# VectorE's list of the MLPs' Strassen groups in another order, and one ScalarE copy moved

## The reference, cut to what matters

```python
h = rmsnorm(x, norm_g[layer, 1]) * (1 + sc2) + sh2
x = x + g2 * (jnp.square(jax.nn.relu(h @ mlp_w1[layer])) @ mlp_w2[layer])
```

## Time and profile before

| what | us |
|---|---|
| median of 3 runs | 1557.08 (1556.45 to 1558.0) |
| the profiled execution | 1556.89 |
| its span, from the first to the last instruction | 1555.1 |
| TensorE's share of the span, by busy time | 98% |
| VectorE, ScalarE, GpSimd | 73%, 44%, 40% |

### The profile page before, as it was taken

How to read it: one execution, slowest core, us unless ns; L and a number is a source line. 1 busy time by engine, 2 the same in 40 slices (tenths; PEclk the granted TensorE clock), 3 DMA queues, 4 the chain that set the end, 5 groups by cost and what they waited for, 6 DMA issues and landing times.

```text
span 1555.1 us, 28369 instructions
## 1 busy us (share of the span) xinstructions
PE 1518.0 (98%) x11754; PEld 1477.0 (95%) x11754; DVE 1139.8 (73%) x1877; ACT 684.3 (44%) x1140; POOL 629.7 (40%) x410
## 2 busy tenths in 40 slices
PE   8999999999999999999999999999999999999998
PEld 7999999999999999999999999999999999999998
DVE  5338678675774787887797888773584698889886
ACT  5323333344442354445355434662442355445553
POOL 0233313314322464665574253101333476567641
PEclk9999999999999999999999999999999999999999
DMA  9454334213233334433535122001222212331222
GB/s 328 160 184 149 115 110 130 96 62 109 82 128 119 112 118 162 147 111 123 177 95 162 35 79 65 28 1 55 82 68 68 82 55 73 104 95 55 81 83 82
DMA packets 123168, 162.20 MB, mean 104 GB/s; under 512 B 4640, under 2 KB 87584, under 8 KB 123040
## 3 DMA queue, kind: packets, MB, share of 16 engines
q1 hardware_dynamic: 121808, 159.34, 32.0%
q10 hardware_dynamic: 1232, 1.05, 0.2%
HBM read 156.44 MB, written 3.93 MB: 103 GB/s over the span
## 4 chain that ended last, share of the span: by engine, by line
PE 72%; DVE 15%; ACT 6%; issue 3%; SPq 2%; DMA 2%; POOL 0%; DVEq 0%; ACTq 0%
PE ps L745 42%; PE ps L1169 19%; DVE fx L2602 3%; PE ps L864 3%; PE ps L1417 2%; DVE held L2616 2%; PE ps L1365 1%; ACT wH L1479 1%; DVE fq L2576 1%; DMA ada<-in_ada_w 1%; SPq L573 1%; DVE ps L2106 1%; PE ps L1001 1%; DVE u L2593 1%; PE ps L1034 1%
## 5 line engine op out<-in xcount | busy, mean ns | idle before, releaser
L2031 POOL TENSOR_TENSOR wL<-raw,wH 128x512 fp32r<-128x512 f32 x188 | 288.0, 1558 | 668.2 <-ACT wH L1461 511.2
L1169 PE MATMUL ps<-fx,wH 128*128 128x320 f32 x1120 | 250.6, 312 | 13.5 <-DVE held L2616 8.7
L745 PE MATMUL ps<-hH,wH 128*128 128x320 f32 x704 | 221.1, 314 | 1.9 <-DVE hL L2117 1.3
L745 PE MATMUL ps<-hH,wL 128*128 128x320 f32 x704 | 217.6, 309 | 0.0
L745 PE MATMUL ps<-hL,wH 128*128 128x320 f32 x704 | 217.5, 309 | 0.0
L1169 PEld LDWEIGHTS ps<-fx,wH 128*128 128x128 f32 x1120 | 185.7, 188 | 21.8 <-issue 14.4
L2031 POOL TENSOR_TENSOR wL<-raw_high,wH 128x512 fp32r<-128x512 f32 x100 | 141.8, 1449 | 115.0 <-ACT wH L1461 115.0
L1169 PE MATMUL ps<-fx,wL 128*128 128x320 f32 x560 | 173.1, 309 | 0.0
L745 PE MATMUL ps<-wH,hH 128*128 128x256 f32 x560 | 162.1, 289 | 2.4 <-DVE hL L2117 2.1
L745 PE MATMUL ps<-wL,hH 128*128 128x256 f32 x560 | 158.3, 283 | 0.0
L745 PE MATMUL ps<-wH,hL 128*128 128x256 f32 x560 | 158.3, 283 | 0.0
(11 more groups left out here) (302 smaller groups left out, 3872.6 us busy)
## 6 DMA issues: line engine op xcount, KB each, us to landing
ada<-in_ada_w SPq DMA_DIRECT2D x40, 1024.0 KB, 5.4
raw<-in_mlp_w SPq DMA_DIRECT2D x64, 512.0 KB, 3.7
raw_high<-in_mlp_w SPq DMA_DIRECT2D x64, 512.0 KB, 3.8
raw<-in_even_w_in SPq DMA_DIRECT2D x28, 512.0 KB, 6.1
pre_w<-in_ada_w SPq DMA_DIRECT2D x16, 512.0 KB, 8.9
raw<-in_odd_w_qkv SPq DMA_DIRECT2D x10, 512.0 KB, 3.6
raw<-in_even_w_out SPq DMA_DIRECT2D x8, 512.0 KB, 3.7
raw<-in_odd_w_o SPq DMA_DIRECT2D x6, 512.0 KB, 3.4
```

What stands on the lines that cost most here:

```text
L745: last = nc.tensor.matmul(ps[:, bank, 0:width], a_, b_, start=(k == 0 and p_ == 0), stop=(k == nk - 1 and p_ == 2))
L1169: last = nc.tensor.matmul(ps[:, bank, 0:HALF], a_, b_, start=(opens and k == 0 and p_ == 0), stop=(k == nk - 1 and p_ == 2), skip_group_ch ...
L2031: last = nc.gpsimd.tensor_tensor(wL[:, at % 4, cs], source(key)[:, cs], wH[:, at % 4, cs].bitcast(F32), ALU.subtract)
```

## The change

Four places of the lists and two of the data change; the number of matmuls, sums, copies and loads stays as it is.

- `strassen_cycle`: VectorE's order between p's low parts and the output of q's block 3 is another. p's T4 is summed after B21's low part and its low part is made four steps later; q's T3 sum stands ahead of the first `combine`; `operand_lo(A11_)` comes before the last two combines, which follow each other directly; the sums S3 and S2 come next and q's T4 sum after them; S1's sum moves from before q's outputs to behind output (2, 0), S4's from between outputs (1, 1) and (1, 2) to behind S1's low part; S1's low part moves behind output (2, 3).
- p's T4 is made in place, `b21 = b21 - t2`, so that the buffer of T2 is free for q's T3 earlier; p's B21 buffer is instead held until T4's low part is made (`source`, `wait_raw_free`, `add_blocks`).
- ScalarE copies q's T3 before F22's relu (`hidden_block(c, F22)`), no longer behind its square.
- TensorE's `part(1)` stands behind p's T1 S1.
- `F_AT` of cycle 7 gives the chunks k = 0 and 1 to the hidden blocks F11 and F21, k = 2 and 3 to F22 and F12, and the rows of `mlp_w2` are loaded to match. In `last_cycle` T4's sum stands behind B21's low part.

```diff
-    return k % 2 + ((2, 0) if k > 1 else (4, 6))[half]
+    return k % 2 + ((4, 6) if k > 1 else (2, 0))[half]
...
+                if key[0] == "p" and key[2] == T4:
+                    return raw(key[:2] + (B21,))
                 return (t24_first if key[0] == "p" else t24_second)[:]
...
-            wait_low(engine, *key)
+            wait_low(engine, *(key[:2] + (T4,) if key[0] == "p" and key[2] == B21 else key))
...
-                part(1)
                 wait_low(pe, "p", s, T1)
                 pe.wait_ge(dve_free, v)
                 for m in range(2):
                     one(T1, S1, m, m)
+                part(1)
...
                         hidden_block(c, F21)
+                        split_product("q", s2, T3, g + 12)
                         hidden_block(c, F22)
-                        split_product("q", s2, T3, g + 12)
...
                         if which == "q":
-                            wait_low(dve, "p", WINO * layer_ + n, T4)
+                            wait_low(dve, "p", WINO * layer_ + n, T2)
+                            wait_source(dve, ("p", WINO * layer_ + n, T4))
...
+                    elif which == "p":
+                        wait_low(dve, which, s, B21)
+                        out, a, b, op = b21, b21, t2, ALU.subtract
...
                     t_lo(s, B22)
+                    t_lo(s, B21)
                     p_add(s, T4)
-                    t_lo(s, B21)
+                    q_add(s2, T3)
+                    combine(c, F11, 0)
+                    q_add(s2, T2)
+                    combine(c, F11, 1)
                     t_lo(s, T4)
-                    combine(c, F11, 0)
-                    q_add(s2, T3)
-                    combine(c, F11, 1)
+                    combine(c, F21, 0)
+                    q_add(s2, T1)
+                    combine(c, F21, 1)
+                    operand_lo(c, A11_)
                     modulate(c, 1)
-                    q_add(s2, T2)
-                    combine(c, F21, 0)
-                    operand_lo(c, A11_)
-                    combine(c, F21, 1)
-                    q_add(s2, T1)
                     combine(c, F22, 0)
+                    combine(c, F22, 1)
                     operand_sum(c, S3_)
-                    combine(c, F22, 1)
+                    operand_sum(c, S2_)
                     q_add(s2, T4)
-                    operand_sum(c, S2_)
-                    operand_sum(c, S1_)
                     operand_lo(c, S2_)
-                    product_out(c, 0, 0)
-                    product_out(c, 0, 1)
+                    for m in range(4):
+                        product_out(c, 0, m)
                     operand_lo(c, S3_)
-                    product_out(c, 0, 2)
-                    product_out(c, 0, 3)
-                    product_out(c, 1, 0)
+                    for m in range(3):
+                        product_out(c, 1, m)
                     operand_lo(c, A22_)
-                    product_out(c, 1, 1)
-                    operand_sum(c, S4_)
-                    product_out(c, 1, 2)
                     product_out(c, 1, 3)
                     product_out(c, 2, 0)
-                    operand_lo(c, S1_)
+                    operand_sum(c, S1_)
                     for m in range(1, 4):
                         product_out(c, 2, m)
+                    operand_lo(c, S1_)
+                    operand_sum(c, S4_)
                     product_out(c, 3, 0)
+                    product_out(c, 3, 1)
                     operand_lo(c, S4_)
-                    for m in range(1, 4):
-                        product_out(c, 3, m)
+                    product_out(c, 3, 2)
+                    product_out(c, 3, 3)
```

More of the change, by code:

```diff
@@ L626, in w2 @@
                     else:
-                        halves = [mlp_w2[layer, 512 * c + 256 * j:512 * c + 256 * (j + 1), 512 * tile:512 * (tile + 1)]
+                        halves = [mlp_w2[layer, 512 * c + 256 * (1 - j):512 * c + 256 * (2 - j), 512 * tile:512 * (tile + 1)]
                                   .rearrange("(k p) n -> p k n", p=P) for j in range(2)]
@@ L2695, in last_cycle @@
                     t_lo(s, B22)
-                    p_add(s, T4)
                     held_out(2)
                     t_lo(s, B21)
+                    p_add(s, T4)
                     held_out(3)
```

## The result

The kernel after takes **1545.65 us** (median of 4 runs, 1544.81 to 1545.77), the one before 1556.78 us beside it: a ratio of 0.9926, 95% interval [0.9909, 0.9943]. The forecast was 1538.0, its range 1531 to 1548: the direction is right and the time lies in the range, but the gain is 11 us where 19 were forecast. The profiled span is 1543.0 us, 12.1 less than the one before.

A forecast was written before the change was run, and what follows sets the result against it. TensorE, busy 1518.0 of 1555.1 us, was taken as the bound, so only its idle time could be won. -25.1 + 1.0 + 5.0 = -19.1 us on 1556.9 gives 1537.8, with 0.2 for the median 1538.0 us; range 1531 to 1548.

The forecast's parts named there:

- The ceiling of 25.1 us: Most the change could win: 22.0 us from three idle spells a cycle, 1.8 from strips, 1.3 from cycle 7.
- second and third spells: TensorE idle 0.24 us inside q's T3 S3 and 0.49 us inside T4 A22 each cycle; both forecast gone.
- the strips' wait: Strips of `ada_w` waiting for their load on TensorE; 1.8 us forecast gone.
- cycle 7's waits: Second matmul of cycle 7 waiting for a chunk, 0.63 us and as much in the other layer; 1.3 us forecast gone.
- The first spell: TensorE idle 1.47 us ahead of q's T2 S2 each cycle; forecast 0.1 a cycle left, 1.0 us over ten.
- The wait at p's T2 S2: New spell in layer 1 from a late T2 sum, 0.4 to 1.2 us a cycle; taken as 1.0, five times.
- X: End of q's T1 S1, three blocks or 10.56 us before p's T2 S2 starts; the clock for the cycle's end.
- I take 1.0, five times: 5.0 us: Forecast cost of the new spell ahead of p's T2 S2 in layer 1's five cycles.
- Its bound of 1.6: Upper bound a cycle at p's T2 S2, if a VectorE low part also falls between T2's two halves.
- its second rival: Waits move in good part: 5.5 us ahead of q's T2 S2, 8.0 layer 1, 3.0 layer 0; 1548.5 us, 16%.
- q's B22: Its load, needed by q's T3 sum ahead of the first combine in layer 0; 1.2 us slack, nothing in the sum.

The follow-up runs named there:

- run 12: Kernel before with the strip behind p's T1 S1, cycle 7's chunks in the other order, and `modulate(c, 1)` behind q's T1 sum: 1553.68 us, 0.9978.
- Run 10: Kernel after with ScalarE's copy of q's T3 back behind F22's square: 1547.26 us, 0.9938.
- Runs 1 and 2: GpSimd's low part of p's B11 cut to 16 of 1024 columns: in the kernel after 1536.57 us, 0.9866; in the kernel before 1556.76 us, 1.0.
- run 3: Kernel before with S4's sum alone moved from between q's outputs (1, 1) and (1, 2) to behind output (2, 3): 1553.09 us, 0.9976.
- run 5: Kernel after with S4's sum moved earlier, between outputs (2, 1) and (2, 2): 1542.71 us, 0.9913.
- Run 7: Kernel after with VectorE waiting for GpSimd's low part of p's T3 before making p's B22's low part: 1543.99 us, 0.9917.
- runs 7 to 9: Kernel after, p's T3 low part before B22's: alone 1543.99 us; with S4's sum behind output (2, 1) 1540.32; that S4 move in layer 1 only 1540.21.

## Why the prediction was right, and where its size was off

- **The ceiling of 25.1 us** came. The second and third spells, the strips' wait and cycle 7's waits are gone in all places. For the last two terms it is the waits that show it; run 12's 3.3 us against 1.8 + 1.3 holds 0.8 us of another.
- **The first spell** was put at 1.0 us in sum and left 2.8: 0.8 in layer 0, 0.4 a cycle in layer 1, inside its bounds of 0 to 0.6 a cycle but near the upper one in layer 1. Run 10 shows the copy of T3 as what remains.
- **The wait at p's T2 S2** was forecast by its place, cause and layer: T2's sum at X + 6.1 to X + 6.9 against X + 5.7. It ended at X + 6.9; 1.0 a cycle was taken, 1.16 measured, 5.8 in all. Runs 1 and 2 show the cause. That the size fits is in part luck: S4's sum ended a microsecond later than reckoned (X - 3.6 instead of X - 4.6), 0.4 of it since it took 1.91 us, not the 1.52 of the earlier trace rows. In run 3 it ends at X - 4.6, as reckoned, and the wait is 0.13, not 1.0. The prediction also followed S4's sum alone to ScalarE, where S1's holds back a copy as well (run 5, `s4_mid`). Layer 0 has no such wait, as forecast.
- **The mis-sized term** is that of the p side, "I take 1.0, five times: 5.0 us", which measured 10.5: 5.8 at T2 S2, 3.9 at T3 S3 (0.97 in four cycles) and 0.8 at B22 S4 in cycle 7, up to which VectorE works without a pause from its late T2 sum on. The prediction looked only at T2 S2. Its bound of 1.6 had VectorE's low part fall between the halves of T2; it fell between those of T3, the block behind. Run 7 shows that with the other order the 0.97 is gone.
- With these numbers the sum is -25.1 + 2.8 + 10.5 = -11.8, and the span fell by 12.1. That is between the forecast and its second rival: 10.5 us on layer 1's p side, where that rival had 8.0, and nothing of its 3.0 in layer 0.
- **q's B22** was reckoned 1.2 us inside its limit in layer 0. The sum waits for it up to 2.5 us in the kernel after, and of that at most 0.47 us of one cycle's first spell and 0.18 us ahead of p's B22 S4 in the same cycle show on TensorE; with T3's low part first (runs 7 to 9) it is on the path in layer 1 too.

## What to carry to other kernels

When a list is ordered by deadlines, follow each moved result through the copy that queues behind it on the next engine and on to the one after: here two sums moved by VectorE came back to VectorE, by way of ScalarE and GpSimd, as slower instructions. Where two engines hold each other up, price every block of the late one, not only the first. Two edits that free a wait can be worth nothing until a third, of another engine's list, goes with them.

## What the runs showed of the hardware that was not expected

- VectorE's sums and low parts and GpSimd's low parts slow each other in both directions: beside GpSimd's B11, T3's sum took 2.31 us instead of 1.23, and GpSimd's two halves 3.12 us instead of 2.54. The Trainium skill (SBUF — State Buffer, section Who interferes with whom) says that a VectorE instruction with two SBUF inputs and a GpSimd instruction that reads SBUF contend, for an exclusive lock. This trace agrees with that, by the same numbers. That T2's sum then follows GpSimd's end at a fixed 3.0 us in four kernels is this case's own number.
- The smallest of these meetings shows the exclusion best. GpSimd's two instructions of 8 columns take 0.37 us together in the cut kernel before, and 1.02 us in the cut kernel after, where VectorE's 0.81 us of A12's low part begin between them (the timelines of GpSimd, in this order):

```profile
1326.85 0.37 POOL L2031 TENSOR_TENSOR wL<-raw,wH 128x8 fp32r<-128x8 f32 x2
```

```profile
1313.86 1.02 POOL L2033 TENSOR_TENSOR wL<-raw,wH 128x8 fp32r<-128x8 f32 x2
```
